# First norm of a streaming encoder step: where the first dense weights load, when the scale and shift rows are turned and copied, and where the fourth row stands

## The reference, cut to what matters

```python
def _rmsnorm(x, g):
    xf = x.astype(jnp.float32)
    y = xf * lax.rsqrt(jnp.mean(xf * xf, axis=-1, keepdims=True) + EPS)
    return (y * g.astype(jnp.float32)).astype(x.dtype)

def _swiglu(h, w_gate, w_up, w_down):
    return (jax.nn.silu(h @ w_gate) * (h @ w_up)) @ w_down

    mod = jax.nn.silu(c) @ w_ada + b_ada
    sh1, sc1, gt1, sh2, sc2, gt2, sh3, sc3, gt3 = jnp.split(mod[:, None, :], 9, axis=-1)

    h = _rmsnorm(x, g_ffn1) * (1 + sc1) + sh1
    x = x + 0.5 * gt1 * _swiglu(h, w1_gate, w1_up, w1_down)
...
```

## Time and profile before

| what | value |
|---|---|
| median of 3 runs | 1281.94 us (1279.59 to 1283.46) |
| the profiled execution's own time | 1274.47 us |
| its span in the trace | 1272.6 us |
| mean granted clock of TensorE | 0.974 of full speed |
| busy PE, DVE, ACT, POOL | 1214.9, 735.0, 369.1, 436.2 us |
| first matmul of the first dense pair | 42.59 us |
| first matmul of unit 2 | 57.48 us |

### The profile page before, as it was taken

How to read it: one execution, slowest core, us unless ns; L and a number is a source line. 1 busy time by engine, 2 the same in 40 slices (tenths; PEclk the granted TensorE clock), 3 DMA queues, 4 the chain that set the end, 5 groups by cost and what they waited for, 6 DMA issues and landing times.

```text
span 1272.6 us, 22847 instructions
## 1 busy us (share of the span) xinstructions
PE 1214.9 (95%) x9027; PEld 1155.9 (91%) x9027; DVE 735.0 (58%) x1113; ACT 369.1 (29%) x576; POOL 436.2 (34%) x204
## 2 busy tenths in 40 slices
PE   4899999999999998999998999999999999999995
PEld 1799999999999997888776778989999999999994
DVE  5688888888675436684884647883232323222224
ACT  4422222222222235552443443341212222211111
POOL 0244444444344333242223202423333333333332
PEclk9799999999999999999999978989999999999998
DMA  9445454544344442122110011213222222222222
GB/s 374 162 153 174 156 172 158 168 161 162 124 134 145 124 139 76 50 66 67 51 57 2 1 42 34 83 51 99 82 83 80 83 79 82 74 78 81 79 81 85
DMA packets 39298, 132.12 MB, mean 104 GB/s; under 512 B 4864, under 2 KB 6032, under 8 KB 37840
## 3 DMA queue, kind: packets, MB, share of 16 engines
q1 hardware_dynamic: 39248, 131.43, 31.3%
HBM read 128.05 MB, written 3.36 MB: 103 GB/s over the span
## 4 chain that ended last, share of the span: by engine, by line
PE 89%; issue 5%; DVE 2%; DMA 2%; ACT 1%; SPq 1%; POOL 0%; DVEq 0%; ACTq 0%; POOLq 0%
PE acc L882 66%; PE acc L1179 10%; PE aux L902 2%; DMA ada_units<-w_ada_units_in 2%; PE acc L921 1%; PE acc L902 1%; PE aux L1086 1%; PE acc L1230 1%; DVE h_lo L1409 1%; PE acc L1262 1%; PE aux L1114 1%; PE aux L1098 1%; PE aux L1034 1%; PE aux L1069 0%; DVE y L1864 0%
## 5 line engine op out<-in xcount | busy, mean ns | idle before, releaser
L420 POOL TENSOR_TENSOR w_lo<-raw,w_hi 128x1024 fp32r<-128x1024 f32 (+2 forms) x182 | 409.9, 2253 | 768.8 <-ACT w_hi L499 768.8
L499 ACT ACTIVATE w_hi<-raw 128x1024 fp32r<-128x1024 f32 (+2 forms) x182 | 175.9, 967 | 727.1 <-PE acc L882 651.7
L882 PE MATMUL acc<-h_hi,w_lo 128*128 128x288 f32 x1312 | 281.3, 295 | 0.0
L882 PE MATMUL acc<-h_hi,w_hi 128*128 128x288 f32 x1312 | 281.1, 296 | 0.0
L882 PE MATMUL acc<-h_lo,w_hi 128*128 128x288 f32 x1312 | 280.7, 295 | 0.0
L882 PEld LDWEIGHTS acc<-h_hi,w_hi 128*128 128x128 f32 x1312 | 211.3, 189 | 0.0
L882 PEld LDWEIGHTS acc<-h_lo,w_hi 128*128 128x128 f32 x1312 | 211.3, 189 | 0.0
L882 PEld LDWEIGHTS acc<-h_hi,w_lo 128*128 128x128 f32 x1312 | 210.7, 188 | 0.0
L1450 DVE CUSTOM_DVE_ANT_0 aux<-ada,cond_all 128x1024 f32<-128x1024 f32 x112 | 186.6, 1666 | 23.8 <-issue 15.3
L882 PE MATMUL acc<-g_lo,w_hi 128*128 128x288 f32 x704 | 151.3, 296 | 0.0
L882 PE MATMUL acc<-g_hi,w_hi 128*128 128x288 f32 x704 | 151.3, 296 | 0.0
(11 more groups left out here) (233 smaller groups left out, 1371.4 us busy)
## 6 DMA issues: line engine op xcount, KB each, us to landing
ada<-w_ada_rows_in SPq DMA_DIRECT2D x56, 512.0 KB, 3.3
raw<-w_gate_in SPq DMA_DIRECT2D x44, 512.0 KB, 3.6
raw<-w_up_in SPq DMA_DIRECT2D x44, 512.0 KB, 3.3
raw<-w_down_in SPq DMA_DIRECT2D x32, 384.0 KB, 3.1
raw<-w_in_in SPq DMA_DIRECT2D x22, 512.0 KB, 3.3
raw<-w_down_in SPq DMA_DIRECT2D x32, 320.0 KB, 2.9
ada_units<-w_ada_units_in SPq DMA_DIRECT2D x8, 1024.0 KB, 16.6
raw<-w_out_in SPq DMA_DIRECT2D x8, 512.0 KB, 3.5
```

What stands on the lines that cost most here:

```text
L420: pool.tensor_tensor(w_lo[:, slot, 0:nk, :], raw[:, slot, 0:nk, :], w_hi[:, slot, 0:nk, :].bitcast(F32), ALU.subtract).then_inc(split, 1)
L499: act.activation(w_hi[:, slot, 0:nk, :], raw[:, slot, 0:nk, :], ACT.Copy).then_inc(rounded, 1)
L882: ins = pe.matmul(acc[:, 2 * b + half, 0:HALF], w[:, slot, n, :], a(k)[:, HALF * half:HALF * (half + 1)], start=first and n == 0 and m == ...
```

## The change

Three lists are written in another order; no instruction is added or removed.

- SP loads the first two weight units (`w1_gate[0]`, `w1_up[0]`) between the second and the third unit of `w_ada_units`; before, they stood between the third and the fourth.
- ACT copies rows 0 and 1 in front of tile 0, row 2 in front of tile 2 and row 3 in front of tile 6, and rounds weight unit 0 in front of tile 0 and unit 1 in front of tile 1.
- PE makes row 0, the mean square, row 1, columns 0, columns 1, row 2, columns 2, and then starts the first dense pair. Row 3 and columns 3 (`last_row`) stand inside the pair, ahead of its step 3.

```diff
--- before.py
+++ after.py
@@ -360,11 +360,11 @@
             load_units(0)
             sp.dma_start(mod[:, :, :], I["b_ada"]).then_inc(small_in, 16)
             sp.dma_start(gains[:, :, :], I["gains"]).then_inc(small_in, 16)
-            for n in (1, 2):
-                load_units(n)
+            load_units(1)
             load(FFN1, 0, I["w1_gate"][0])
             load(FFN1 + 1, 1, I["w1_up"][0])
-            load_units(3)
+            for n in (2, 3):
+                load_units(n)
             sp.dma_start(cond_all[:, :, :].rearrange("p s k -> p (s k)"), I["cond_row"].to_broadcast([P, 2 * D])).then_inc(cond_row_in, 16)
             load_pair(0)
             load_ffn(1, FFN1, DOWN1)
@@ -536,12 +536,12 @@
                 if n:
                     round_next(first + 2, 0)
                 for k in range(KD):
-                    if n == 0 and k % 2 == 0:
-                        act.wait_ge(row_made, k // 2 + 1)
-                        act.activation(start_row[:, k // 2 % 2, :], aux[:, 2 + k // 2 % 2, :], ACT.Copy).then_inc(row_kept, 1)
-                        if k == 4:
-                            for s in range(2):
-                                round_next(s, s)
+                    if n == 0:
+                        for row in {0: (0, 1), 2: (2,), 6: (3,)}.get(k, ()):
+                            act.wait_ge(row_made, row + 1)
+                            act.activation(start_row[:, row % 2, :], aux[:, 2 + row % 2, :], ACT.Copy).then_inc(row_kept, 1)
+                        if k < 2:
+                            round_next(k, k)
                         act.wait_ge(shift_ready, k // 2 + 1)
                     if n and k == 2:
                         round_next(first + 3, 1)
@@ -884,11 +884,13 @@
                                             start=first and n == 0 and m == 0, stop=last and n == len(ks) - 1 and m == 2)
                 ins.then_inc(used, 1)
 
-            def product_pair(u, arrived, before, hi, lo, place=acc, order=tuple(range(KD))):
+            def product_pair(u, arrived, before, hi, lo, place=acc, order=tuple(range(KD)), beside=None):
 
 
 
                 for step in range(KD + LAG):
+                    if beside and step == 3:
+                        beside()
                     for b, at_k in ((0, step), (1, step - LAG)):
                         if not 0 <= at_k < KD:
                             continue
@@ -951,7 +953,7 @@
                 pe.wait_ge(silu_ready, done + SPARE)
                 pe.wait_ge(g_full, done + SPARE)
                 if n == 1:
-                    product_pair(first, h_ready, 0, tokens(h_hi), tokens(h_lo))
+                    product_pair(first, h_ready, 0, tokens(h_hi), tokens(h_lo), beside=last_row)
                     hidden(1)
                 else:
                     unnormed_pair(2, first)
@@ -991,8 +993,8 @@
                                     start=True, stop=True)
                 ins.then_inc(start_sum, 1)
 
-            pe.wait_ge(cond_ready, 1)
-            for n in range(KD // 2):
+            def start_rows(n):
+
                 if n >= 2:
                     pe.wait_ge(row_kept, n - 1)
                 for k in range(KD):
@@ -1002,11 +1004,20 @@
                     ins = pe.matmul(aux[group, 2 + n % 2, :], scond[:, k, :], ada_units[:, n, k, :],
                                     start=(k < 4), stop=(k >= 4), skip_group_check=True)
                 ins.then_inc(row_made, 1)
-                if n == 0:
-                    mean_square(0)
-                else:
-                    start_columns(n - 1)
-            start_columns(KD // 2 - 1)
+
+            def last_row():
+
+                start_rows(3)
+                start_columns(3)
+
+            pe.wait_ge(cond_ready, 1)
+            start_rows(0)
+            mean_square(0)
+            start_rows(1)
+            start_columns(0)
+            start_columns(1)
+            start_rows(2)
+            start_columns(2)
             ffn(1, FFN1, DOWN1)
```

## The result

| | before | changed |
|---|---|---|
| median, 20 runs each | 1280.62 us (1273.76 to 1285.27) | 1271.24 us (1266.74 to 1278.51) |
| profiled execution's own time | 1274.47 us | 1272.95 us |
| its span, granted clock | 1272.6 us, 0.974 | 1271.2 us, 0.978 |

The ratio of changed to before is 0.9942, 95% interval 0.9925 to 0.9959: some 7.4 us less, 0.6%.

What follows compares the result with a forecast made beforehand. PE, busy 95% of the span, bounds the kernel. The pair starts 10.4 us earlier; row 3 with copy and columns 3 (4.3), a hole (0.4) and PE's wait (1.3) leave 4.5: 1277.4 us, range 1274.0 to 1281.3.

Steps and rivals of the forecast that it cites:

- Parts 1 to 4: Start up to the dense pair (loads, ACT, DVE against POOL, PE): pair starts near 32.15 us instead of 42.6.
- Part 3: DVE against POOL: they exclude one another, POOL's subtractions cost `start_mod(0)` 3.6 us, so it ends at 32.0.
- Part 5: Row 3 inside the pair at the high clock: columns 3 end at 41.2, PE waits 1.3 us, unit 2 at 53.0.
- the first rival: Rival, chance 0.15: POOL stays out of DVE's way in `start_mod(0)`; unit 2 at 51.0, 6.5 us less, 1275.4.
- the second: Rival, chance 0.25: PE's clock rises only behind row 3; unit 2 at 55.1, 2.4 us less, 1279.5.
- The sum: Start of unit 2 moves from 57.48 to 53.0, 4.5 us less; 1270.0 for the profiled execution, 1277.4 from the median.
- so I cost the rest at nothing: Behind unit 2: weight unit 3 comes in time and DVE's lateness is covered, so no further loss, 0 us.
- up to 1 us: Behind unit 2: the bound on the further loss if DVE's cover were missing.
- each microsecond by which that instant moves should reach the end: Behind the start of unit 2: PE is the limit, so the whole shift there, 4.5 us, shows in the time.
- taking the same difference from the median: Whole kernel: the profile's 4.5 us taken from the median, 1281.94 - 4.5 = 1277.4, though the profile stood 7.5 us below.
- The third: Rival, chance 0.04: the broken dense pair keeps the low clock; with all 78 matmuls slow, 4.5 us later, 1286.4.
- The fourth: Rival, chance 0.06: the gain is taken back by a later stage with a timetable of its own; 1281.9.

Runs made afterwards that it cites:

- nolock: Changed kernel, but POOL writes zeros instead of subtracting for the low halves of the first two weight units: 1270.21 us, ratio 0.9952.
- a_2: The changed kernel again, no edit, for a second trace: unit 2 at 53.5 us, `z` begins at 464.9.
- a_3: The changed kernel again, no edit: 1274.26 us, ratio 0.9955 to the kernel before.
- e_row3first: Changed kernel with row 3 and columns 3 ahead of the dense pair instead of inside it: 1274.27 us (nine runs), ratio 0.9977.
- e_table: Changed kernel without ACT's second Silu table load ahead of the rounding of unit 2: 1274.77 us, ratio 0.9986.
- v_sp: Changed kernel with each weight load in SP's first-network list between the two loads of `ada`, not behind both: 1271.39 us, ratio 0.9947.
- b_4: The kernel before again, no edit, for its trace: unit 2 at 57.8 us.
- skip28: Kernel before, leaving out 28 of the 96 matmuls of weight units 2 and 3: 1271.86 us, ratio 0.9971.
- add28: Changed kernel, making 28 of the matmuls of units 2 and 3 twice: 1276.44 us, ratio 0.9986.
- v2: Changed kernel with new SP order, one table load less, both weight units loaded ahead of unit 1, earlier roundings, columns 0 before row 1: 1270.86 us, ratio 0.9938.

## Why the prediction was wrong in its size

Three steps failed. The third put the time below the range; the first two nearly cancel.

**Parts 1 to 4 held.** The pair started at 32.66, forecast 32.15; the clock rose near 36.5, forecast 36.6. (One reading is off by 0.1: half of the 1.81 from 45.20 is 3.3 us behind 42.77, not 3.4. Nothing hangs on it.) Part 3 put POOL on `start_mod(0)`, which it then held for 1.8 and 1.3 us: tile 0's first instruction started at 26.61, and `low_tile` 1 took 2.29 and ended at 32.7, forecast 32.0. nolock prices the whole at 3.2 us of DVE's time, forecast 3.6. Who was stopped first was another in this execution and in a_2: not a scaled tile of 2.5 to 3 us but the four-column scale ahead of it; in a_3 it was the tile. That an instruction of 0.16 us can pay 2.00 was shown already by the earlier trace rows for an addition of the same size. The Trainium skill ("SBUF — State Buffer", section "Who interferes with whom") says that the lock is held for the whole instruction, and that issue order and not shape decides who blocks; this case's trace agrees with both (2.00 for 0.16), and nolock shows its other half, that POOL's writing alone holds nothing up.

**Part 5 held.** Row 3 ran at the high clock (1.92, forecast 2.1), its copy kept PE waiting for 1.29 (1.1), columns 3 ended at 41.62 (41.2), ACT began to round unit 2 at 49.45 (49.05), PE waited 1.42 for POOL (1.3), and unit 2 started at 53.55 (53.0). The forecast had the first rival at 51.0 and the second at 55.1. e_row3first shows that this part carries the gain, nolock that part 3 is its largest brake.

**The first step that failed is the last one of "The sum": "so I cost the rest at nothing".** Behind unit 2 came a hole of 1.44 us at unit 4 (2.0 in a_2). I had followed weights 3 from ACT to PE and not the load of unit 4 in SP's list, where it stands behind two loads of `ada` that wait for DVE's products; those start behind ACT's silu, at 48.62 (49.73 before), so they came 1.1 us earlier where unit 2 came 4.0 earlier, and two of them were stretched from 1.23 to 3.2 us beside POOL. That a product can be stretched so stood in the trace of before, at the place where I had read only POOL's 2.75:

```profile
65.81 3.24 DVE L1450 CUSTOM_DVE_ANT_0 aux<-ada,cond_all 128x1024 f32<-128x1024 f32 x1
```

My bound "up to 1 us" was too small as well. e_table made the hole larger and v_sp took it away. The statement ahead of the sum, that behind unit 2 "each microsecond by which that instant moves should reach the end", fails by the same 1.4 to 2.0 us.

**The second is the base: "taking the same difference from the median".** The 4.5 us were read against a unit 2 at 57.48, the earliest of the five executions traced (middle one 58.5). The first rise of PE's clock falls early in some of them and late in others, and POOL's subtractions hit DVE's `start_mod(2)` in the kernel before accordingly: its scale and first tile lost 0.05 us where the rise was earliest, 0.45 in b_4, and 1.2 to 2.2 in the three executions with a late rise. Against the middle execution the changed kernel gains 5.0 at unit 2 and, after the hole at unit 4, 3.2 at `z`. The two errors nearly cancel: the forecast's 4.5 stands against the 3.6 between the lower group and the changed kernel.

**The third made the miss: that a difference at the start is the same in all executions.** The median that was measured lies 6.2 us under the forecast. Of these, 1281.94 - 1280.62 = 1.3 is the median of three runs, two of them long, against that of twenty. The rest is 9.4 by the two medians of twenty against my 4.5. By the counts it goes to how the executions divide: the kernel before has a third of its runs in the group near 1283, which pulls its median up and is 2.6 us of its mean, and the changed kernel has none there: its longest of 33 runs is 1280.49. Part of it is the luck of the draw: ten of those twenty runs were long, against 57 of 162 in all, and their median of 1280.62 falls into the gap, where no run lies. Over all runs the medians are 1276.6 (162) and 1272.0 (33), some 4.5 us apart; that this is the forecast's difference is luck in part, since the first two errors cancel. From a base of 1276.6 the forecast would have been 1272.1. I read the scatter of 1279.59 to 1283.46 as noise round one value; it was the upper group and the gap below it, while the profile, at 1274.47, was of the lower. Both numbers were in front of me, and "It stands 7.5 us below the median" was noted and not followed up: such a distance, more than the whole gain in dispute, says that two kinds of execution are being compared.

**The rivals.** The first did not occur (nolock puts its price at unit 2 at 1.7 us, forecast 2.0). The second did not (row 3 at the high clock). The third did not. The fourth, the gain taken back by a timetable of its own, occurred in part, in the first network: 1.4 to 2.0 us. None of them had a gain above the first rival's 6.5, and so the range ended at 1274.0.

**Open.** Why the changed kernel has so few long executions is not known. The 5.8 us between the groups lie in the mixer, 600 us behind the change, in a stretch where PE's clock falls and comes back later in one group than in the other. Forty matmuls at the start (warm_before) left four of twelve runs above 1281 in the kernel before, an instant moved by 4 us (skip28) left its two groups, e_row3first had no long execution with unit 2 at 58.3, and add28, with 28 matmuls more, lost 2.2 us beyond its instants. That the place of the clock's falls in the mixer hangs on the instants of what comes before is a guess. In the `z` stage the same hole, whose end lies between 646.2 and 654.9 us in the traces, sometimes costs 1.5 us and sometimes nothing, and the instant does not tell which.

## What to carry to other kernels

Before a gain of a few microseconds is costed, look whether the profiled execution lies where the median lies; if not, find the second group first, and price the change in each. When an early stage is shortened, follow every queue that feeds what comes next up to the load that issues it: here SP's list held unit 4 behind loads that waited for DVE. And a subtraction on POOL should be put where DVE waits or runs what was seen to pass beside it (here the reciprocals), for in other places it costs up to its whole length. Having one SBUF input is not enough to be safe, as the CAST shows. Last, a hole on PE can cost more than its length when the clock falls behind it, as in e_table.

## What the runs showed of the hardware that I had not expected

- A VectorE instruction over four columns with two SBUF inputs took 2.00 us instead of 0.16 beside POOL's subtraction, and the custom product with two SBUF inputs 3.22 and 3.25 instead of 1.23. The reciprocals, with one, took 3.77 for two with or without a subtraction of 2.35 beside them (v2), but a CAST of 128x576, also with one, took 1.84 instead of 0.46.
- Behind a hole on PE of 2.67 us near 66 us the clock was granted at 0.57 for the next 4 us (e_table), behind holes of 1.44 and 1.99 us at the same place at 1.00 (the changed kernel's first profile, a_2).
- The clock fell behind a hole of 1.94 us near 650 us in some executions of a kernel and not in others (0.67 and 1.00 of full speed in the 4 us behind it), for 1.5 us of the time.
- Forty dummy matmuls raised the clock before row 0 (1.07 instead of 1.94 for half a row), but it had fallen again by 18.0 us in one of the two kernels, and neither kernel became faster; the loads came about 1 us later in both.
- One and the same program on one core fell into two groups of times, 7.4 us apart; of the 9.0 us between a trace of each, 5.8 lay between the end of `z` and the third norm.
